# Gate rows of two recurrences: broadcast transfers in place of TensorE spreads

## The reference, cut to what matters

```python
bcum = jnp.cumsum(lfc, axis=1)
lw = jnp.where(tri, bcum[:, :, None] - bcum[:, None, :] + lic[:, None], -jnp.inf)
m_t = jnp.maximum(l_prev, jnp.max(lw, axis=2))
sc = jnp.einsum('bthd,bshd->btsh', qc, kc) * jnp.exp(lw - m_t[:, :, None])
...
h = num / jnp.maximum(jnp.abs(den), jnp.exp(-m_t))[..., None]
```

## Time and profile before

| | |
|---|---|
| median of 3 runs | 1395.98 us (1392.22 to 1397.54) |
| profiled execution, its own time | 1394.52 us |
| its span in the trace | 1392.8 us |
| TensorE matmuls, busy | 1309.9 us, 94% of the span |
| DVE, ACT, POOL busy | 44%, 31%, 15% |
| mean granted TensorE clock | 0.963 of full speed |
| DMA | 182.54 MB, 131 GB/s over the span |

### The profile page before, as it was taken

The page is one execution under the profiler, slowest core; times in us unless marked ns, Lnnn a source line. Parts: engine busy times, 40 slices in busy tenths (PEclk is TensorE's granted clock), DMA queues, the critical chain, the costliest instruction groups (busy, mean ns, idle before and its releaser), DMA issues.

```text
span 1392.8 us, 22346 instructions
## 1 busy us (share of the span) xinstructions
PE 1309.9 (94%) x6932; PEld 1075.2 (77%) x6932; DVE 608.9 (44%) x1335; ACT 427.1 (31%) x1029; POOL 211.8 (15%) x388
## 2 busy tenths in 40 slices
PE   5999998899999999979989999988999999999797
PEld 4877776668888888867877868776787888888586
DVE  3253135425665555552223611434365555555612
ACT  0131234115444444430013212421153444444300
POOL 0000041000033333300000001400012333331000
PEclk9999999789999999997999999988999999999899
DMA  7444331115255444401474433301162444444032
GB/s 289 154 126 162 104 124 57 63 50 184 100 167 167 166 166 166 167 31 61 151 282 146 158 125 100 130 8 63 61 227 71 165 161 164 162 163 158 31 113 100
DMA packets 80984, 182.54 MB, mean 131 GB/s; under 512 B 15579, under 2 KB 50148, under 8 KB 69494
## 3 DMA queue, kind: packets, MB, share of 16 engines
q1 hardware_dynamic: 59014, 100.25, 21.3%
q0 software_dynamic: 17280, 72.90, 15.7%
q10 hardware_dynamic: 4608, 8.39, 1.6%
HBM read 167.59 MB, written 13.90 MB: 130 GB/s over the span
## 4 chain that ended last, share of the span: by engine, by line
PE 76%; issue 11%; DMA 5%; DVE 3%; SPq 3%; ACT 1%; POOLq 1%; POOL 1%; DVEq 0%; ACTq 0%
PE ps L512 20%; PE ps L621 20%; PE ps L966 9%; PE ps L608 3%; DMA ring<-in_weights 2%; PE ps L715 2%; PE ps L723 2%; SPq L302 2%; DMA states<-in_mlC 2%; PE ps L639 2%; PE ps L599 1%; PE ps L761 1%; PE ps L580 1%; PE ps L541 1%; PE ps L533 1%
## 5 line engine op out<-in xcount | busy, mean ns | idle before, releaser
L621 PE MATMUL ps<-wk,scr 128*128 128x258 f32 x2048 | 468.3, 382 | 0.0
L621 PEld LDWEIGHTS ps<-wk,scr 128*128 128x128 f32 x2048 | 379.1, 190 | 53.0 <-issue 3.1
L512 PE MATMUL ps<-uT,ring 128*128 128x264 f32 (+1 forms) x1344 | 315.2, 399 | 7.5 <-DMA ring<-in_weights 7.5
L512 PEld LDWEIGHTS ps<-uT,ring 128*128 128x128 f32 (+1 forms) x1344 | 252.8, 194 | 65.6 <-issue 10.3
L1290 DVE TENSOR_REDUCE ssq<-scr 128x4 f32<-128x512 f32 x256 | 170.8, 682 | 156.3 <-ACT scr L1038 155.2
L1038 ACT ACTIVATE scr<-ps 128x512 f32<-128x512 f32 x256 | 151.7, 593 | 5.6 <-DVE ssq L1290 5.6
L449 POOL DMA_DIRECT2D kr<-in_krope x256 | 134.8, 528 | 88.6 <-issue 75.7
L423 POOL DMA_DIRECT2D ring<-in_weights x64 | 34.7, 543 | 655.2 <-PE ps L512 454.3
L1035 ACT ACTIVATE raws<-ps 128x4 f32<-128x4 f32 x256 | 44.2, 173 | 284.8 <-PE ps L621 284.7
L966 PE MATMUL ps<-pt,ring 128*128 128x264 f32 x512 | 120.7, 399 | 3.6 <-DVEq L1735 3.6
L966 PEld LDWEIGHTS ps<-pt,ring 128*128 128x128 f32 x512 | 99.9, 196 | 21.4 <-DVEq L1735 4.0
(11 more groups left out here) (315 smaller groups left out, 1307.6 us busy)
## 6 DMA issues: line engine op xcount, KB each, us to landing
ring<-in_weights POOLq DMA_DIRECT2D x60, 1024.0 KB, 5.2
lat<-in_lat SPq DMA_DIRECT2D x256, 128.0 KB, 3.0
rows<-rowscr SPq DMA_DIRECT2D x16, 1024.0 KB, 7.3
lat<-in_weights SPq DMA_DIRECT2D x8, 1024.0 KB, 6.7
kr<-in_krope POOLq DMA_DIRECT2D x256, 32.0 KB, 2.2
uT<-in_memv SPq DMA_DIRECT2D x16, 512.0 KB, 5.5
uT<-in_memk SPq DMA_DIRECT2D x16, 512.0 KB, 5.6
states<-in_ssm SPq DMA_DIRECT2D x16, 256.0 KB, 4.1
```

The lines of the kernel that those rows point to most:

```text
L512: last = mm(ps[part, bank, 0:T], w[:, k, 0:ROPE] if m == KR else w[:, k, :], u3[:, k, :], start=k == 0, stop=k == KT - 1)
L621: last = mm(ps[:, 1 + 2 * (j % 2) + half, 0:258], latT[:, g % 2, q, c, :], wk[:, 2 * c + half, at:at + 258], start=c == 0, stop=c == 1)
```

## The change

The gate rows are written to a small buffer in device memory, `gatescr`, and read back by broadcast transfers: eight rows of `acum` into `states` (as `acB`, 1 MB over all partitions), four of `nmx` into free tiles of `pt` (`nmB`, 0.5 MB), four of `mT` into `emm` (0.5 MB). `seg` reads these, ACT's `exp(-m)` works in place in `emm`, and all spreads are gone. As `acB` lies in `states`, the first sample's states are loaded after the recurrences.

```diff
-def spread_bank(n):
-    return (0, 1, 4, 5)[n % 4] if n < 8 else n % 2
...
+        gatescr = nc.dram_tensor("gatescr", (16, SEQ), F32, kind="Internal").ap()
+        acB = states[:, :, :, :].rearrange("p u s n -> p (u s n)").rearrange("p (h t) -> p h t", h=8)
+        nmB = pt[:, GATE:GATE + 4, :].rearrange("p a t -> p (a t)")[:, 0:4 * SEQ].rearrange("p (h t) -> p h t", h=4)
...
                 load_big(l, R_MK, 1)
-                load_states(l, 0, 0, 0)
...
                 load_tables()
+                sp.wait_ge(*g_scan(l, 1))
+                for at, row, n in ((0, acum, 8), (8, nmx, 4), (12, mT, 4)):
+                    sp.dma_start(gatescr[at:at + n], row[0:n, 0:SEQ]).then_inc(gs_saved.sem, 16)
...
+                def load_gate_rows(to, at, n, done):
+                    sp.dma_start(to, gatescr[at:at + n].rearrange("h t -> (h t)").partition_broadcast(P)
+                                 if to.shape[1] != n else
+                                 gatescr[at:at + n].partition_broadcast(P)).then_inc(done.sem, 16)
+
+                sp.wait_ge(*gs_saved(l, 48))
+                for u in range(2):
+                    sp.wait_ge(*st_saved[u](l, 0))
+                load_gate_rows(acB, 0, 8, ac_in)
                 sp.wait_ge(*n_out(l, 3))
...
                 sp.wait_ge(*n_in(l, 3))
+                load_gate_rows(nmB, 8, 4, nm_in)
                 load_latents(0, places, 0, PAGES // 2)
...
+                sp.wait_ge(*conv_saved(l, 16))
+                sp.wait_ge(*tok_mm(l, 7))
+                load_gate_rows(emm, 12, 4, mt_in)
                 sp.wait_ge(*pre_row(l, 2))
...
                 load_latents(0, high, PAGES // 2, PAGES)
+                load_states(l, 0, 0, 0)
                 sp.wait_ge(*fin_out(l, 1))
...
                 pe.wait_ge(*pre_row(l, 2))
-                for n in range(3):
-                    spread(l, n)
                 masked(l, 1)
-                ahead = 3
                 for n in range(12):
                     recur(l, n)
...
-                    while ahead < 12 and ahead <= (n + 3 if n < 5 else n + 2):
-                        spread(l, ahead)
-                        ahead += 1
...
-                pe.wait_ge(*seg_out(l, 12))
-                pe.wait_ge(*em_out(l, 4))
...
+                    if n == 8:
+                        act.wait_ge(*mt_in(l, 16))
                     if n >= 8:
-                        fn(emm[:, n - 8, :], ps[:, n % 2, 256:512], ACT.Exp, scale=-1.0).then_inc(em_out.sem, 1)
+                        fn(emm[:, n - 8, :], emm[:, n - 8, :], ACT.Exp, scale=-1.0).then_inc(em_out.sem, 1)
...
-                dve.wait_ge(*bc_mm(l, n + 1))
+                if n % 8 == 0:
+                    dve.wait_ge(*(nm_in if n else ac_in)(l, 16))
...
+                row = acB[:, n] if n < 8 else nmB[:, n - 8]
+                ts(dec[:, n % 4, 0:256], row, cols[:, 0, c:c + 1], 0.0, op, ALU.min)
+                ts(dec[:, n % 4, 256:384], row[:, P:256], cols[:, 1, c:c + 1], 0.0, op, ALU.min
```

More of the change, by code:

```diff
@@ L251, in build @@
         st_mm, st_out = sig("masked_mm", 6), sig("masked_out", 6)
-        bc_mm, seg_out, seg_exp, seg_w, ry_mm = (
-            sig(f"rec_{x}", 12) for x in ("bc", "seg", "exp", "weights", "y"))
+        seg_out, seg_exp, seg_w, ry_mm = (sig(f"rec_{x}", 12) for x in ("seg", "exp", "weights", "y"))
+        gs_saved, ac_in, nm_in, mt_in = sig("gate_rows_saved", 48), sig("acum_in", 16), sig("nmx_in", 16), sig("m_in", 16)
         ry_out, em_out = sig("rec_out", 8), sig("rec_emm", 4)
@@ L569, in masked @@
                 mm(ps[:, 6, 256:384], k[:, P:256], q[:, P:256], start=True, stop=True).then_inc(st_mm.sem, 1)
[L571 to L583, removed]
             def recur(l, n):
@@ L1259, in seg @@
                 c, op = (n, ALU.subtract) if n < 8 else (24 + n - 8, ALU.add)
-                ts(dec[:, n % 4, 0:256], ps[:, spread_bank(n), 0:256], cols[:, 0, c:c + 1], 0.0, op, ALU.min)
-                ts(dec[:, n % 4, 256:384], ps[:, spread_bank(n), P:256], cols[:, 1, c:c + 1], 0.0, op, ALU.min
+                row = acB[:, n] if n < 8 else nmB[:, n - 8]
+                ts(dec[:, n % 4, 0:256], row, cols[:, 0, c:c + 1], 0.0, op, ALU.min)
+                ts(dec[:, n % 4, 256:384], row[:, P:256], cols[:, 1, c:c + 1], 0.0, op, ALU.min
                    ).then_inc(seg_out.sem, 1)
```

## The result

The changed kernel takes 1362.67 us (median of 4 runs, 1357.34 to 1368.72), beside 1394.1 us for the kernel before in the same runs. The ratio of the runs is 0.9749, with a 95% interval of 0.9707 to 0.9792 (the quotient of these two medians is 0.9775), so it is 2 to 3% faster. Two of the four runs lie near 1368 us at a granted clock of 0.966, where the other two have 0.975 and 0.976; what lowered it is not known. The profiled execution took 1357.34 us, with a span of 1355.5 us: 37.3 us less than the span before. The sum of the prediction, which is made between profiled executions, had 28.4.

A forecast was written before the change was run, and what follows sets the result against it. TensorE's own list was taken as the path. Per layer 12.23 (start and spreads) + 2.38 (half rate) - 0.4 (state load) = 14.21 us, 28.4 for both; 1394.5 - 28.4 = 1366.1 us, range 1357 to 1375.

The forecast's parts named there:

- Start: Start of each layer's recurrences: without the first three spreads, step 0 starts 1.16 us earlier, `masked(1)` 1.03 us earlier.
- Second half-rate stretch: TensorE behind the gap before step 7: half rate gone, `masked(4)` 0.79 and the tile 1.59 less, 2.38 us a layer.
- rival 1: The half-rate stretch behind step 7 stays: 2 x 2.38 us is not gained, 1370.9 us; chance 0.14.
- DVE keeps up: In the recurrences, TensorE never waits for DVE from step 0 to 11: taken as 0, at most 6.3 us a layer.
- Rivals 3 and 6: 3: DVE paces five steps without a tile, 1372.4 us, chance 0.07; 6: no gain for the path, 1394.5 us, chance 0.03.
- The broadcasts: Three transfers of gate rows land well before they are needed: price 0 unless they push a ring chunk TensorE awaits.
- The moved state load: First sample's states loaded behind the recurrences, ahead of `rows`: costs 0.4 us a layer, bounds 0 and 3.7.
- Rival 4: First sample: `rows` land 3.7 us later and TensorE waits as long, 3.3 us more a layer, 1372.7 us; chance 0.04.
- The steps' spreads: Spreads removed from TensorE, per layer: steps 3-4 2.30 us, 5-7 1.86, 8 2.81, 9 2.00, 10-11 2.10.
- The first half-rate stretch stays in the sum: Early recurrences: half rate behind the gap before step 0 remains, since that gap stays at 2.5 us; no gain counted.
- rival 2: The early half-rate stretch goes too: steps 0 and 1 and the tile shorten, 3.3 us a layer, 1359.4 us; chance 0.12.
- Rival 5: Clock stays at 1.2 GHz through the recurrences: 31.9 us more in each layer, 1429.9 us; chance 0.03.

The follow-up runs named there:

- the second set of runs: The changed kernel again, five rounds, nothing edited: 1358.1 us (1355.49 to 1360.47), ratio 0.9727 to the kernel before.

## Why the prediction was right, and where its sum was off

The forecast of 1366.1 us lies 3.4 above the median and inside the runs; 1362.67 lies inside its range. Faster was its likely case, by 28.4 us or 2.0%. That the median lies so near is in part luck: these medians differ by 31.4 us, those of the second set of runs (1396.96 and 1358.1) by 38.9, the spans by 37.3. The mechanism was right, and the sum was too small. By its own steps:

- **What bounds the kernel**: right. TensorE's list was the path; 36.8 of the 37.3 us of span came out of the two stages.
- **Start**: 1.16 forecast, 1.15 measured, as two small errors cancel. `masked(1)` follows its mask after 0.15 us (265.77 to 265.92) and not 0.05, so it comes 0.94 and not 1.03 us earlier; the chain behind it is 0.21 shorter and not 0.13, since two `seg` stand in it. `seg` was to take 0.35 us and does.
- **Second half-rate stretch**: right. With the gap inside the block, 5.65 for 5.60 and 1.68 for 1.59. The spreads kept as unread work showed that the gap was its cause, so rival 1 falls.
- **DVE keeps up**: right, but for step 1: DVE's multiplication for it is done at 270.13 (269.58 + 0.55), and step 1 starts at 270.18, some 0.1 us late, and so behind step 0 and not beside it. No later step waits for DVE. Rivals 3 and 6 fall.
- **The broadcasts**: right; doubling them costs nothing. The first is issued at 139.72 and lands 6.5 us later, long before step 0.
- **The moved state load**: 0.4 a layer forecast. Alone it costs TensorE 0.94 us in one layer and nothing in the other, so the size was right there; in the changed kernel TensorE has no such wait. Rival 4, with 3.3 us more a layer, falls. The Trainium skill's rule that all issuing engines share the same 16 DMA engines (DMA: Bandwidth & Descriptors, section Issuing engines are not separate DMA queues) is not tested by the delay of `rows`, as the states and `rows` are issued by one engine, SP.
- **The steps' spreads, mis-sized**: "Steps 5 to 7, at full rate ... three times 1.86" priced the spread alone, three times 0.62. A spread also stood between two steps that run side by side without it. The two pairs give 1.56 us more in each layer (2 x 0.78, from two steps of 0.79 or 0.80 to 0.81 for both). The rows of before hold no two neighbouring state-space steps, so this had no row, and the sum had no bound for it either.
- **"The first half-rate stretch stays in the sum"**: half wrong. The gaps before it stay, but it begins later and ends earlier: steps 0 and 1 take 0.54 us less than the spreads' going explains, the tile 0.97 less. That is 1.5 of the 3.3 us that rival 2 would have had.
- **Shape changes**, not in the sum: blocks that meet a product of their own shape are some 0.1 us shorter, 0.7 us a layer in all, taken as what is left.

These three make 1.56 + 1.51 + 0.73 = 3.8 us a layer, all of 18.41 - 14.61. With the 0.4 of the state load, which the sum took off and the changed kernel did not pay, the two stages give 28.4 + 2 x 4.2 = 36.8 us; the profiled executions differ by 37.2.

The margins of the range were misread by a little: the kernel before ran 2.3 us below and 3.0 us above its profiled execution, not 2 and 2.5 us. It decides nothing here.

Rival 5 (the clock stays down) is refuted: the granted clock of the recurrences went from 0.86 to 0.96, that of the span from 0.963 to 0.975. The Trainium skill's rule that the throttled clock is the default and activity releases it (TensorE: Matmul & The Clock Gate, section Part 1: The HAM clock gate (the "warmup" mystery)) was read too simply there. Fewer products did not lower the clock: with the wait before step 7 gone and the spreads kept, the two stages have 0.88 and 0.91, with both gone 0.96, and with the waits at the start filled 1.00. The rule does not contradict these numbers. The clock of the whole span says less: the six runs without waits at the start have 0.972 to 0.978, the nine of the changed kernel 0.966 to 0.976.

## What to carry to other kernels

Price a removed instruction together with what it stood between: once it is gone its neighbours may run side by side, or follow one another without a change of shape. A wait of TensorE can cost more than its own length, by the half-rate stretch behind it: filling the two waits at the start, 4 us, with a long product that is due anyway gained 8 us a layer here, of which some 1.7 were half rate and 1.6 two new pairs of neighbours. And try a small move of work alone, and follow the delay to the engine that is the path: of 1.3 us a layer at DVE, 0.94 us in one layer of two came through to TensorE.

## What the runs showed of the hardware that was not expected

- Two fp32 products of 128 rows by 64 columns on opposite halves of the array: two whole steps in 0.81 us, against 1.45 on the same half.
- A product behind one of another shape takes 0.65 to 0.70 us where it takes 0.59 behind its own; a tile 3.83 against 3.73.
- The half rate came up again at the first sample's keys (4.92 us for 3.65) in the kernel that had more time at full rate ahead of it. The waits ahead of these keys are the same, 1.24 and 0.78 us; why the clock fell behind them here, and neither before nor in the kernel that writes both heads to the same half, is not settled.
